# Slots of w_out freed row by row, four loads ahead of the number of passes, own positions for expert 0, and seeds moved, in a hybrid block with 32 experts

## What is computed

```python
merged = merged + jax.nn.sigmoid(h @ w_merge_gate[l, n]) * (y_b @ w_branch[l, n])
x = x + merged @ w_out[l]
h2 = rms_norm(x, norm_ffn[l])
x = x + hier_moe(h2, ...)
```

## Time and profile before

| what | value |
|---|---|
| median of 3 runs | 712.26 us (711.34 to 715.14) |
| profiled execution | 712.9 us |
| its span, first to last instruction | 711.1 us |
| mean granted TensorE clock | 0.894 |
| PE busy, share of the span | 587.2 us, 83% |
| PEld busy | 410.9 us, 58% |
| DVE busy | 302.8 us, 43% |
| ACT busy | 189.7 us, 27% |
| queue q1 (SP's loads) | 245.44 MB, 85.6% of 16 engines |
| mean rate over the span | 348 GB/s |

### The profile page before, as it was taken

How to read it: one execution, slowest core, us unless ns; L and a number is a source line. 1 busy time by engine, 2 the same in 40 slices (tenths; PEclk the granted TensorE clock), 3 DMA queues, 4 the chain that set the end, 5 groups by cost and what they waited for, 6 DMA issues and landing times.

```text
span 711.1 us, 15452 instructions
## 1 busy us (share of the span) xinstructions
PE 587.2 (83%) x6636; PEld 410.9 (58%) x6636; DVE 302.8 (43%) x626; ACT 189.7 (27%) x332; POOL 29.6 (4%) x56
## 2 busy tenths in 40 slices
PE   8999999999999999996875767776678656887584
PEld 5787899999999885553432333333334333443342
DVE  6475976985474945442222222122312222111412
ACT  4493355473535434110111001010011100110111
POOL 8003000000000020000000000000000000000000
PEclk9999999999999999998798788797877988687969
DMA  8995546536579699999999999999999999999993
GB/s 253 349 328 187 163 137 203 175 121 213 175 274 420 234 395 369 427 425 428 425 427 425 426 429 427 426 427 427 425 425 428 427 427 427 424 426 427 423 417 146
DMA packets 39619, 247.73 MB, mean 348 GB/s; under 512 B 4360, under 2 KB 6496, under 8 KB 25472
## 3 DMA queue, kind: packets, MB, share of 16 engines
q1 hardware_dynamic: 38096, 245.44, 85.6%
q0 software_dynamic: 912, 1.25, 1.0%
q10 hardware_dynamic: 544, 0.06, 0.1%
HBM read 245.67 MB, written 1.06 MB: 347 GB/s over the span
## 4 chain that ended last, share of the span: by engine, by line
PE 50%; DMA 44%; SPq 1%; another core or an unknown queue 1%; DVE 1%; issue 1%; ACT 0%; ACTq 0%; DVEq 0%
DMA wide<-in_w_expert_up 38%; PE ps L1366 8%; PE ps L1029 6%; PE ps L1030 6%; PE ps L1031 6%; DMA wide<-in_w_expert_down 3%; PE ps L1401 3%; PE ps L1002 3%; PE ps L1004 3%; PE ps L1003 3%; PE ps L1325 2%; DMA ring<-in_w_in 2%; PE ps L1413 1%; PE ps L1381 1%; SPq L526 1%
## 5 line engine op out<-in xcount | busy, mean ns | idle before, releaser
L1366 PE MATMUL ps<-wide,xe 128*32 128x256 f32 x2048 | 162.1, 470 | 109.3 <-DMA wide<-in_w_expert_up 109.3
L1366 PEld LDWEIGHTS ps<-wide,xe 128*32 128x32 f32 x2048 | 75.9, 131 | 176.9 <-issue 132.1
L1882 DVE TENSOR_TENSOR xe<-ps,g_ffn 128x256 f32<-128x256 f32 x32 | 13.6, 425 | 258.4 <-PE ps L1334 258.4
L1486 DVE TENSOR_TENSOR ring_lo<-ring,w_hi 128x1024 fp32r<-128x1024 f32 x76 | 92.0, 1228 | 46.2 <-ACT w_hi L721 45.7
L721 ACT ACTIVATE w_hi<-ring 128x1024 fp32r<-128x1024 f32 x76 | 79.0, 1058 | 58.8 <-PE ps L1031 35.3
L1029 PE MATMUL ps<-hT_hi,w_hi 128*128 128x256 f32 x320 | 89.4, 279 | 0.2 <-DVE hT_lo L1498 0.2
L1030 PE MATMUL ps<-hT_lo,w_hi 128*128 128x256 f32 x320 | 88.4, 276 | 0.0
L1031 PE MATMUL ps<-hT_hi,ring_lo 128*128 128x256 f32 x320 | 88.4, 276 | 0.0
L925 ACT ACTIVATE he<-ps 128x128 f32<-128x128 f32 x32 | 8.9, 278 | 207.7 <-PE ps L1381 204.7
L1401 PE MATMUL ps<-wide,he 128*32 128x256 f32 x1024 | 62.5, 382 | 1.9 <-DMA wide<-in_w_expert_down 1.8
L1029 PEld LDWEIGHTS ps<-hT_hi,w_hi 128*128 128x128 f32 x320 | 60.1, 188 | 0.7 <-issue 0.7
(11 more groups left out here) (276 smaller groups left out, 785.9 us busy)
## 6 DMA issues: line engine op xcount, KB each, us to landing
wide<-in_w_expert_gate SPq DMA_DIRECT2D x27, 2048.0 KB, 45.6
wide<-in_w_expert_up SPq DMA_DIRECT2D x27, 2048.0 KB, 48.2
wide<-in_w_expert_down SPq DMA_DIRECT2D x27, 2048.0 KB, 41.1
ring<-in_w_in SPq DMA_DIRECT2D x8, 2048.0 KB, 16.1
ring<-in_w_merge_gate SPq DMA_DIRECT2D x6, 2048.0 KB, 9.6
wide<-in_w_expert_gate SPq DMA_DIRECT2D x10, 1024.0 KB, 13.2
wide<-in_w_expert_up SPq DMA_DIRECT2D x10, 1024.0 KB, 10.6
wide<-in_w_expert_down SPq DMA_DIRECT2D x9, 1024.0 KB, 11.8
```

What stands on the lines that cost most here:

```text
L1366: ins = t_.matmul(ps[q * WIN:(q + 1) * WIN, b, 0:QW], xe[b][:, k % 2, k // 2, :], w, start=(k == 0), stop=(k == KD - 1))
L1486: v.tensor_tensor(piece(ring_lo, g, c), piece(ring, g, c), by_row(out_hi[g == 19][c]).bitcast(F32), ALU.subtract).then_inc(wpre_lo, 1)
```

## The change

SP: loads 12 and 14 wait for a signal in the middle of out_half(1), 16 and 17 for one behind the low x high matmuls of their quarter of tile 1, which now come first. Loads 22 to 25 are issued ahead of the wait for npass. TensorE: the four calls of `seed`, two quarters each, become eight of one quarter, put at other places; the last is before turn_rows(0, 0). Expert 0's positions come from six matmuls of one column (`first_spot`) over `first`, a comparison of the chosen experts with expert 0; the 14 matmuls for all experts come after turn_rows(0, 0). DVE: in_group(0) and best_two(0) come before x1_add(1, 2); pick_w for expert 0 comes before `below`; rows_in(0, 0) before the slots and choose(0, 1). ACT: the table is copied after expert 0's rows.

```diff
+N_AHEAD = 4
+        first = place("first", [P, TT, TOPK], BF16)
...
-                elif n < 16:
+                elif n in (12, 14):
+                    sp.wait_ge(chunk_done, chunks_before[NPRE - 2] + 1)
+                elif n in (13, 15):
                     sp.wait_ge(proj_done, first_bank[NPRE - 2] + 2)
-                elif n in (16, 18):
+                elif n == 16:
+                    sp.wait_ge(chunk_done, chunks_before[NPRE - 2] + 2)
+                elif n == 18:
                     sp.wait_ge(proj_done, first_bank[NPRE - 2] + 4)
+                elif n == 17:
+                    sp.wait_ge(chunk_done, chunks_before[NPRE - 2] + 3)
...
-            for n in [0, 1, 2, 3, 11] + list(range(4, 11)) + [12, 13, 14, 15, 16, 18, 17, 19, 21, 20]:
+            for n in [0, 1, 2, 3, 11] + list(range(4, 11)) + [12, 14, 13, 15, 16, 18, 17, 19, 21, 20]:
                 first_load(n)
+            def next_load(n, done):
+                if n not in paired:
+                    sp.wait_ge(unit_free, done + (UNITS + free_at(n - RING)))
+                elif n % 2 == 0:
+                    sp.wait_ge(unit_free, done + (UNITS + max(free_at(n - RING), free_at(n + 1 - RING))))
+                load_unit(n)
+            for n in range(RING, RING + N_AHEAD):
+                next_load(n, 0)
             sp.wait_ge(route_ready, 1)
...
             rows_copy(0, 0)
+            act.wait_ge(slot_ready, 1)
+            s_.activation(flat(tab[:, :, :]), ps[:, 3, 2 * NE:4 * NE], ACT.Copy).then_inc(table_ready, 1)
...
+                elif tt == TT - 1:
+                    ins.then_inc(chunk_done, 1)
...
+                if tt and ks[0] == 0:
+                    for k in range(KD):
+                        ins = t_.matmul(o, merged_hi[:, k, rows], wl[k], start=(k == 0), stop=False)
+                    ins.then_inc(chunk_done, 1)
...
-            out_quarter(1, 1, range(0, 4))
+            out_quarter(1, 1, range(0, 2))
             turn_x1(1, range(4, 6), 4)
             turn_x1(0, range(6, KD), 5)
-            out_quarter(1, 1, range(4, 6))
+            out_quarter(1, 1, range(2, 6))
             route(0, range(6, KD), 5)
             out_quarter(1, 1, range(6, KD))
             route(1, range(4, 6), 4)
             turn_x1(1, range(6, KD), 6)
+            seed(0, 0)
             route(1, range(6, KD), 6)
-            seed(0, 0)
+            seed(0, 2)
+            seed(1, 0)
+            seed(1, 2)
             seed(0, 1)
+            seed(0, 3)
...
+            pe.wait_ge(assign_ready, 1)
+            for k in range(TOPK):
+                first_spot(tri_bf[:, :], 0, k, 0, start=(k == 0), stop=False)
+                first_spot(ones_bf[:, :], 0, k, 1, start=False, stop=False)
+                ins = first_spot(tri_bf[:, :], 1, k, 1, start=False, stop=(k == TOPK - 1))
             ins.then_inc(pos_mm, 1)
+            seed(1, 1)
...
-            seed(1, 0)
             pe.wait_ge(xn0_ready, 1)
             pe.wait_ge(xn1_ready, 1)
             pick_rows(0, 0)
+            seed(1, 3).then_inc(seeded, 1)
             turn_rows(0, 0)
-            seed(1, 1).then_inc(seeded, 1)
+            all_spots()
...
             group_of(0)
+            in_group(0)
+            best_two(0)
             x1_add(1, 2)
             square_sum(1, 2)
             mean_square(1)
-            in_group(0)
             scale_out(1)
-            best_two(0)
             group_of(1)
             in_group(1)
             best_two(1)
+            v.tensor_tensor(first[:, :, :], iota_f[:, 0:1].unsqueeze(1).broadcast_to([P, TT, TOPK]), ie8[:, :, 0:TOPK],
+                            ALU.is_equal).then_inc(assign_ready, 1)
...
+            dve.wait_ge(pos_mm, 1)
+            for tt in range(TT):
+                ins = v.scalar_tensor_tensor(out=pick_w[0][:, tt, :], in0=iota_w[:, :], scalar=ps[:, 2, tt:tt + 1],
+                                             in1=stat[:, 44 + tt:45 + tt].broadcast_to([P, WIN]), op0=ALU.is_equal, op1=ALU.mult)
+            ins.then_inc(chosen_ready, 1)
...
             dve.sem_inc(same_ready, 1)
+            rows_in(0, 0)
+            slots()
             dve.wait_ge(table_ready, 1)
             choose(0, 1)
-            rows_in(0, 0)
```

More of the change, by code:

```diff
@@ L582, in _ @@
                         load_unit(n)
[L583 to L588, removed]
+                    for n in range(RING, RING + N_AHEAD):
+                        next_load(n, UNITS * p)
+                for n in range(RING + N_AHEAD, UNITS):
+                    next_load(n, UNITS * p)
             for tt in range(TT):
@@ L891, in _ @@
             s_.activation(rt[:, :, 3:4], rt[:, :, 2:3], ACT.Exp).then_inc(e2_ready, 1)
-            act.wait_ge(slot_ready, 1)
-            s_.activation(flat(tab[:, :, :]), ps[:, 3, 2 * NE:4 * NE], ACT.Copy).then_inc(table_ready, 1)
             def rows_copy(i, e):
@@ L1225, in out_quarter @@
                 o = bank(2 * q + tt)[:, 0:QW]
+                wl = [ring_lo[19 % PRE_RING][:, UNIT * q + QW * k:UNIT * q + QW * (k + 1)] for k in range(KD)]
+                if tt and ks[0] == 0:
+                    for k in range(KD):
+                        ins = t_.matmul(o, merged_hi[:, k, rows], wl[k], start=(k == 0), stop=False)
+                    ins.then_inc(chunk_done, 1)
                 for k in ks:
@@ L1230, in out_quarter @@
                     wh = out_hi[1][c][:, QW * (k % 4):QW * (k % 4 + 1)]
-                    wl = ring_lo[19 % PRE_RING][:, UNIT * q + QW * k:UNIT * q + QW * (k + 1)]
-                    t_.matmul(o, merged_hi[:, k, rows], wh, start=(k == 0), stop=False)
-                    t_.matmul(o, merged_hi[:, k, rows], wl, start=False, stop=False)
+                    t_.matmul(o, merged_hi[:, k, rows], wh, start=(tt == 0 and k == 0), stop=False)
+                    if tt == 0:
+                        t_.matmul(o, merged_hi[:, k, rows], wl[k], start=False, stop=False)
                     ins = t_.matmul(o, merged_lo[:, k, rows], wh, start=False, stop=(k == KD - 1))
@@ L1243, in turn_x1, with seed @@
                 ins.then_inc(x1_turned, 1)
[L1245 to L1250, removed]
+            def seed(tt, q):
+                return t_.matmul(bank(4 + q, 2)[:, tt, :], ident[:, :], x_tok[:, tt, QW * q:QW * (q + 1)],
+                                 start=(tt == 0), stop=False, skip_group_check=True)
             def route(tt, ks, copied):
@@ L1299, in spots, with first_spot, all_spots @@
                                  skip_group_check=True, **flags)
[L1301 to L1308, removed]
-            ins.then_inc(pos_mm, 1)
+            def first_spot(lhsT, tt, k, at, **flags):
+                return t_.matmul(ps[:, 2, at:at + 1], lhsT, first[:, tt, k:k + 1], skip_group_check=True, **flags)
+            pe.wait_ge(assign_ready, 1)
[3 more added lines that the diff above has]
+                ins = first_spot(tri_bf[:, :], 1, k, 1, start=False, stop=(k == TOPK - 1))
+            ins.then_inc(pos_mm, 1)
+            seed(1, 1)
+            def all_spots():
+                for tt in range(TT):
+                    pe.wait_ge(assign_ready, 3)
+                    for k in range(TOPK):
+                        spots(ones_bf[:, :], below[:, tt, k, :], 0, 3, start=(tt == 0 and k == 0), stop=False)
+                        spots(tri_bf[:, :], eh[:, tt, k, :], tt, 1, start=False, stop=False)
+                        if tt == 0:
+                            spots(ones_bf[:, :], eh[:, 0, k, :], 1, 1, start=False, stop=False)
+                        ins = spots(ones_bf[:, :], eh[:, tt, k, :], 3, 1, start=False, stop=(tt == 1 and k == 1))
+                ins.then_inc(pos_mm, 1)
             def rows(values, ready, b):
@@ L1842, in _ @@
             best_two(1)
+            v.tensor_tensor(first[:, :, :], iota_f[:, 0:1].unsqueeze(1).broadcast_to([P, TT, TOPK]), ie8[:, :, 0:TOPK],
+                            ALU.is_equal).then_inc(assign_ready, 1)
+            dve.wait_ge(assign_ready, 1)
+            link(v.tensor_tensor(stat[:, 44:46].unsqueeze(2), first[:, :, 0:1], first[:, :, 1:2], ALU.add))
             every = iota_f[:, :].unsqueeze(1).unsqueeze(1).broadcast_to([P, TT, TOPK, NE])
@@ L1853, in _, with slots @@
             dve.sem_inc(now_ready, 1)
-            dve.wait_ge(assign_ready, 2)
-            link(v.tensor_tensor(stat[:, 44:46].unsqueeze(2), eh[:, :, 0, 0:1], eh[:, :, 1, 0:1], ALU.add))
-            dve.wait_ge(pos_mm, 1)
+            dve.wait_ge(assign_ready, 3)
             spot = ps[:, 3, 0:2 * NE].rearrange("p (t e) -> p t e", e=NE)
[L1858 to L1866, removed]
+            def slots():
+                dve.wait_ge(pos_mm, 2)
+                for k in range(TOPK):
+                    ins = v.tensor_tensor(hits[:, :, k, :], eh[:, :, k, :], spot, ALU.mult)
+                link(ins)
+                v.tensor_reduce(slotf[:, :, :], hits[:, :, :, :], AX_X, ALU.add).then_inc(slot_ready, 1)
+                dve.wait_ge(slot_ready, 1)
```

## The result

| what | before | after |
|---|---|---|
| median | 712.26 us (9 runs) | 719.69 us (9 runs, 716.76 to 720.2) |
| ratio after to before | | 1.0086, 95% interval 1.007 to 1.0102 |
| profiled execution, its span | 712.9, 711.1 us | 720.1, 718.3 us |

The change made the kernel 7 us slower, where 2 us faster was forecast. The range ended at 713.4 us, so the time lies outside it.

What follows compares the result with a forecast made beforehand. The second half was taken as bound by the weight stream at some 425 GB/s. A gain of 2.6 us less 0.6 for a later load's thin margin took 712.9 to 710.9, so a median of 710.3 us; range 708.3 to 713.4.

Steps and rivals of the forecast that it cites:

- w_out row by row: End of out_half: loads 12 and 14 go 5.5 us earlier, 3.5 us of DMA idle gone, at no cost to TensorE.
- the sum: Total of the forecast's terms: a gain of 2.6 us less 0.6, so 2.0 us, with 6.9 us idle in all.
- reading (b): DMA stream: the slowest engine was never idle after 247 us, so its first gap moves everything behind it; gain 2.6 us.
- the first gap: DMA stretch from 244 to 250 us at 175 GB/s against 427: 3.5 us of idle time, expected to close.
- the pair 22/23: Weight loads whose start ends the last gap: forecast to go at 273.45 instead of 274.20 and land at 281.1 instead of 283.7.
- reading (a): DMA stream: all 16 engines ran dry before the pair 22/23, whose landing moves with its issue; gain 0.75 us; rival's chance 0.27.
- the 2.6 us: Forecast gain in the landing of the pair 22/23, 281.1 instead of 283.7 us, by reading (b).

Runs made afterwards that it cites:

- the early seeds: Three seeds put ahead of the last turn, on the changed kernel with `first` over a dead tile and VectorE's order as changed: 711.19 us, ratio 0.9986.

## Why the prediction was wrong

**The step that failed.** In "w_out row by row" the prediction said: the number of matmuls is the same everywhere, so TensorE pays nothing. In the sum this term stood at nothing; it measured 5.3 us alone. It counted instructions and took their pace from the trace of before. The line that declares `first` was listed as part of the change and never priced; it moves the operands of more than a thousand matmuls. Shown by adding it alone (+5.3 us), by taking it away from the changed kernel (-7.4), and by keeping it with 480 bytes more (-7.4). No rival had this mechanism, and no range from the routing stretch could hold it.

The pace in the traces agrees. The table gives the mean time from start to start of the 256-column matmuls on hT, ya and yg, some 1155 in each trace, without the steps over 0.135 us.

| tokens' operands | start to start, us | median, us |
|---|---|---|
| in place (kernel before) | 0.1136 | 712.3 |
| 32 bytes up, unused tile | 0.1183 | 717.8 |
| 32 bytes up, changed kernel | 0.1183 | 719.7 |
| 64 bytes up | 0.1198 | 719.1 |
| 128 bytes up | 0.1174 | 718.2 |
| 256 bytes up | 0.1136 | 712.7 (one run) |
| 512 bytes up | 0.1139 | 712.2 (one run) |
| weights and tokens 32 bytes up | 0.1136 | 712.7 |

An estimate from it: 1155 times 0.0047 us are 5.4 us for 32 bytes, beside the 5.3 measured.

**The sum.** It was built on reading (b), that the slowest DMA engine never ran dry after 247, so that the first gap's 3.5 us would move everything behind it. Its rows were right but for one reading: of loads 12 to 15 only 12 and 13 went at 246.84, 14 and 15 at 247.69. The inference was not right. The loads alone gained nothing, with the first gap closed; and without the loads ahead the time went with the issue of the pair 22/23. Of the two, reading (a) fits: the end comes some 436 us behind that issue. Its premise, that all engines had run dry, is seen in the trace of the changed kernel (0 GB/s from 276 to 278) and not in the trace before. One row was also less firm than it looked: the pair landed 9.5 us behind its issue before, and in seven versions that share its order of loads 8.0 to 9.8 us behind it, so part of the 2.6 us lay in one execution. The Trainium skill's rule of separate rings ("DMA: Bandwidth & Descriptors", Queues, rings and completion order) isn't contradicted by this; that an engine's lag carries its gain to the end is what I made of it. Landing behind a later issue doesn't prove that an engine had work all the time.

**VectorE's order.** x1_add(1, 2) was expected 1.2 us late. In the changed kernel it came 1.27 us behind the end of the quarters (269.39 and 268.12), where it had been 0.07 us behind it before (262.50 and 262.43): 1.2 us late, as expected. The version with 512 bytes has the dense pace of before and kept the clock, so its profile can be laid beside the prediction's times (VectorE, then TensorE):

```profile
263.72 0.42 DVE L1810 TENSOR_TENSOR x_tok<-x_tok,ps 128x256 f32<-128x256 f32 x1
```
```profile
268.78 1.07 PE L1364 MATMUL ps<-xn,pick_w 128*32 128x256 f32 x16
...
271.54 1.93 PE L1405 MATMUL ps<-wide,xe 128*32 128x256 f32 x32 [0.27 <-DVE xe L1929]
```

Forecast were 263.7 for x1_add(1, 2), 268.8 for pick_rows, 271.5 for the first gate_up and 273.45 for the pair 22/23, which went at 273.55. So the count of this stretch was good in the one profile of this order that has the old dense pace and kept the clock. Its span is 1.7 us below that of before, but the median of the version's ten runs is 712.26: over the executions the gain isn't there.

**What it did not have at all** is the clock. The prediction says that VectorE waits there, but not that TensorE does, for 1.4 us, with 2.4 us of seeds in line behind. In the profiled execution the fall cost 2.2 us on the seeds and put the small positions 2.2 us behind `first`. With the old order the wait is 0.44 us and no run of 12 was above 710.6.

**The parts, by the runs.** Shift of the dense operands: +5.3 us alone, 7.4 taken from the whole. Why the two differ is not shown; the medians may hold different shares of executions with the fall. Loads' part: nothing by itself; the four loads ahead are worth 2.4 us when the routing is early enough for npass to be late. Small positions, seeds' new places and all_spots with the old order: 709.92 against 713.08 with the loads alone, -3.2 us. VectorE's new order: +2.4 us on the median; how much of it is the longer wait and how much the clock is open, since the early seeds kept the clock in their profile and brought only 1.1. The version that beats both kernels is the changed one with `first` over a dead tile and the old order, 0.38% below the kernel before (0.25% to 0.5%).

**Open.** Why the place matters: that the distance from the weights counts is shown, and that 256 and 512 bytes of shift are harmless where 32, 64 and 128 are not. Which accesses meet (TensorE's two reads, or its reads and what the loads and VectorE write into the ring) and which places between would be good, was not tried. The times at 256 and 512 bytes rest on one run each and its profile; the changed kernel 512 bytes up has ten. Also open is what decides whether the clock falls after the wait of 1.4 us. Of four profiles with this wait, the clock fell in two (the changed kernel and the one with `first` over a dead tile) and stayed in two (128 and 512 bytes up). The four have the same instructions in the same order and differ in addresses, and each has one profile, so that the addresses decide isn't excluded.

## What to carry to other kernels

A new tile is an edit to every tile placed behind it: look at the starts of matmuls far from the change, not at their durations, and put small new tiles over dead ones (tried here) or behind the large ones (not tried). With a ring of slots, closing an early gap of the DMA engines can merely move it, as here; ask which issue is the last one to come out of a dry queue and price the change by that issue first. An engine order that makes TensorE wait costs the wait and, in some profiles here, a time at half the clock for the work behind it.

## What the runs showed of the hardware

- In matmuls of 128 x 128 weights and 256 float32r columns, the start-to-start time was 0.1137 us with the tokens' operands at their old distance from the weights and 0.1183 us with 32 bytes more, at a granted clock of 1.00 in both. Shifts of 32, 64 and 128 bytes were slow (0.117 to 0.120 us), 256 and 512 fast (0.114), and 32 bytes for weights and tokens together fast (0.114). The Trainium skill ("SBUF — State Buffer", Operand start alignment) wants a start at a multiple of the element's size, and says that it speaks of legality and that nothing was timed; all these places are legal, and the runs here show that they differ in speed.
- Over the whole kernel before, this was worth 5.3 to 6.4 us of 712.
- After a wait of 1.4 us for VectorE, TensorE's granted clock was 0.50 in two profiles and 1.00 in two others, of kernels with the same instructions at other addresses; five seeds took 4.1 and 4.6 us in the first two and 2.4 in the others.
- The pair 22/23, one load of 2048 KB, landed 8.0 to 9.8 us behind its issue in the profiles of eight kernels that issue their loads in the same order (9.5 in the kernel before).
